# All pages of cached values issued from GpSimd's queue, two per unit behind the visit that frees the ring

## The reference

```python
def fox_sample(q, k_new, v_new, logf_new, cache_k, cache_v, cache_logf, page_table):
    DB, DS = q.shape[:2]
    P = page_table.shape[1] * PAGE_SIZE
    k_past = cache_k[page_table].reshape(DB, P, N_HEADS, HEAD_DIM)
    v_past = cache_v[page_table].reshape(DB, P, N_HEADS, HEAD_DIM)
    ...
    s = jnp.einsum('bqhd,bkhd->bhqk', q, k_all, preferred_element_type=jnp.float32) * HEAD_DIM ** -0.5
    s = s + (Fh[..., P:, None] - Fh[..., None, :])
    ...
    p = jax.nn.softmax(s, axis=-1)
    out = jnp.einsum('bhqk,bkhd->bqhd', p.astype(v_all.dtype), v_all)
    return out.reshape(DB, DS, ATTN_WIDTH)
```

## Time and profile before

| what | value |
|---|---|
| three runs | 1341.45 us median (1341.02 to 1342.53) |
| the profiled execution | 1339.1 us, its span 1337.3 us |
| TensorE busy | 1295.2 us, 97% of the span |
| VectorE, ScalarE, GpSimd busy | 689.0, 401.7, 607.0 us |
| granted TensorE clock | 0.993 over the span |
| cached values, issues from SyncE | 256 of 256 KB, 3.3 us median from issue to landing |

### The profile page before, as it was taken

How to read it: one execution, slowest core, us unless ns; L and a number is a source line. 1 busy time by engine, 2 the same in 40 slices (tenths; PEclk the granted TensorE clock), 3 DMA queues, 4 the chain that set the end, 5 groups by cost and what they waited for, 6 DMA issues and landing times. The chain is left out here.

```text
span 1337.3 us, 21207 instructions
## 1 busy us (share of the span) xinstructions
PE 1295.2 (97%) x7573; PEld 1035.9 (77%) x7573; DVE 689.0 (52%) x1049; ACT 401.7 (30%) x589; POOL 607.0 (45%) x286
## 2 busy tenths in 40 slices
PE   8999999999899999999999999999999999999996
PEld 6889898988799976777777777677777776666675
DVE  4765555534577654636446384645545234321438
ACT  3546666664521341121212112121211202112016
POOL 1027877753400438565666655676672112121114
PEclk9999999999999999999999999999999999999999
DMA  7344545330254157777687867778685544567633
GB/s 243 104 145 150 170 158 158 127 99 1 89 188 152 36 161 252 256 258 238 232 262 244 279 225 246 237 239 281 198 288 168 200 137 175 191 267 282 236 128 127
DMA packets 111538, 255.02 MB, mean 191 GB/s; under 512 B 12624, under 2 KB 22737, under 8 KB 106048
## 3 DMA queue, kind: packets, MB, share of 16 engines
q1 hardware_dynamic: 102152, 246.99, 54.9%
q10 hardware_dynamic: 8320, 4.19, 1.1%
q0 software_dynamic: 960, 2.47, 0.6%
HBM read 243.72 MB, written 10.12 MB: 190 GB/s over the span
## 5 line engine op out<-in xcount | busy, mean ns | idle before, releaser
L886 POOL TENSOR_TENSOR WL<-WR,WH 128x1024 fp32r<-128x1024 f32 x55 | 133.0, 2419 | 336.3 <-ACT WH L1122 336.3
L794 POOL TENSOR_TENSOR AR<-AR,QB 128x1024 f32<-128x1024 f32 x96 | 235.1, 2465 | 107.5 <-DMA AR<-cache_k 93.4
L1548 PE MATMUL PSM<-XH,WH 128*128 128x512 f32 x672 | 213.4, 399 | 0.0
L1548 PE MATMUL PSM<-XL,WH 128*128 128x512 f32 x672 | 208.0, 391 | 0.0
L1548 PE MATMUL PSM<-XH,WL 128*128 128x512 f32 x672 | 207.0, 389 | 0.0
L2139 DVE TENSOR_TENSOR ACC<-ACC,PSM 128x512 f32<-128x512 f32 x160 | 108.6, 684 | 133.5 <-PE PSM L1558 133.1
L1122 ACT CAST WH<-WR 128x1024 fp32r<-128x1024 f32 x55 | 57.6, 1049 | 354.2 <-PE PSM L1548 186.0
L1548 PEld LDWEIGHTS PSM<-XH,WH 128*128 128x128 f32 x672 | 121.9, 188 | 50.4 <-issue 27.6
L1558 PE MATMUL PSM<-R 128*128 128x512 f32 x528 | 148.4, 390 | 0.1
L1548 PEld LDWEIGHTS PSM<-XH,WL 128*128 128x128 f32 x672 | 126.2, 188 | 27.3
L1548 PEld LDWEIGHTS PSM<-XL,WH 128*128 128x128 f32 x672 | 126.1, 188 | 27.3
(11 more groups left out here) (281 smaller groups left out, 2187.7 us busy)
## 6 DMA issues: line engine op xcount, KB each, us to landing
AR<-cache_v SPq DMA_DIRECT2D x256, 256.0 KB, 3.3
AR<-cache_k SPq DMA_DIRECT2D x192, 256.0 KB, 3.5
AR<-ws SPq DMA_DIRECT2D x37, 1024.0 KB, 6.4
WR<-ffn SPq DMA_DIRECT2D x66, 512.0 KB, 4.9
WR<-w_in SPq DMA_DIRECT2D x20, 512.0 KB, 4.7
ACC<-cache_k SPq DMA_DIRECT2D x32, 256.0 KB, 2.8
WR<-cache_k SPq DMA_DIRECT2D x32, 256.0 KB, 3.1
WR<-w_o SPq DMA_DIRECT2D x5, 1024.0 KB, 5.1
```

The source lines that it names most:

```text
L794: pool.tensor_tensor(keys, keys, QB[:].rearrange("p (o n) -> p o n", o=1).to_broadcast([P, KP, AW]), ALU.mult).then_inc(k_mul, 1)
L886: pool.tensor_tensor(lo, WR[:, raw_weight(e), :], hi.bitcast(F32), ALU.subtract).then_inc(ffn_lo, 1)
L1548: ins = pe.matmul(out[:, hc], (hi, lo)[a][:, k * P:(k + 1) * P], x[b][:, k, hc], start=(k == 0 and n == 0), stop=(k == KC - 1 and n == 2))
```

## The change

SyncE's program loses all issues of values. GpSimd's program gets them: `value_pages(n, first)` reads two page numbers of chunk n, waits for `v_used` to reach n - 1 (from the third chunk on), and issues the two DMAs. `VPAGE` places four such calls behind each visit, one in each of the next four units: two for the first of the two chunks, two for the second. In a unit they stand behind the rests and ahead of the multiply. The first two chunks (four calls) go out behind the rests of the first two weight tiles. 128 calls stand in GpSimd's program in all.

```diff
-VLOAD = tuple(o + n for o in VALUES for n in (1, 2))
+VPAGE = {b * WIN + o + 1 + n: (b * NCH + 2 * i + 2 + n // 2, 2 * (n % 2)) for b in range(NB) for i, o in enumerate(VALUES)
+         for n in range(CH) if b * NCH + 2 * i + 2 < NB * NCH}
...
             sp.wait_ge(o_free, HRT * OC)
-            pages(0, VR, 0, t["cache_v"], v_ld)
-            pages(1, VR, 1, t["cache_v"], v_ld)
             sp.wait_ge(wo_lo, OC + 1)
...
-                if u == (NB - 1) * WIN + VLOAD[-1]:
+                if u == (NB - 1) * WIN + VALUES[-1] + 2:
                     stream_tile(2)
...
-                for c in range(2, NCH + 2):
-                    n = b * NCH + c
-                    if o == VLOAD[c - 2] and n < NB * NCH:
-                        pages(n, VR, n % 2, t["cache_v"], v_ld, v_used, n - 1)
...
+            def value_pages(n, first):
+
+                numbers = [pool.value_load(page[0:1, bass.ds(n * CH + j, 1)], min_val=0, max_val=POOL_PAGES - 1)
+                           for j in (first, first + 1)]
+                if n >= 2:
+                    pool.wait_ge(v_used, n - 1)
+                for j, p in enumerate(numbers, first):
+                    pool.dma_start(VR[n % 2][:, j * AW:(j + 1) * AW],
+                                   t["cache_v"][bass.ds(p, 1), :, :].rearrange("a p n -> (a p) n")).then_inc(v_ld[n % 2], 16)
+
+            pool.wait_ge(o_free, HRT * OC)
+            for n in range(2):
+                for first in (0, 2):
+                    value_pages(n, first)
             for u in range(UNITS):
                 for e in range(2, len(WORDER)):
                     if WORDER[e][2] + 1 == u:
                         rest(e)
+                if u in VPAGE:
+                    value_pages(*VPAGE[u])
                 if u in KMUL:
                     multiply(EARLY + KMUL.index(u))
```

## The result

The changed kernel takes 1363.32 us (median of 4 runs, 1359.79 to 1366.24) against 1341.24 us for the kernel before, measured beside it: a ratio of 1.0167 (95% interval 1.0136 to 1.0198), **22 us slower**. The forecast was 1340.2 us, in a range from 1338.4 to 1362. The profiled execution took 1364.32 us around a span of 1362.6 us, 25.3 us more than before.

The account below looks back on a forecast made before the run. TensorE was taken to bound the kernel: 2.9 us of its stalls for cached values go, 1.4 + 0.2 come, net 1.3 us gained, so 1340.2 us on the median's scale. Whole range 1338.4 to 1362, the forecast's own 1338.5 to 1342.5.

Parts of the forecast that it names:

- The bound and what there is to gain: TensorE, 485 to 1100 us: only its delays cost time; two waits for late pages of values, 2.9 us at most.
- Price of an issue: GpSimd's queue: 0.62 us a page, between 0.542 and 1.03; at about 0.7 the new stalls reach 2.9 us.
- GpSimd's load: GpSimd, per period of 50 units: 32 pages add 19.8 us to 49.6, making 69.4 of 78 us, 89%.
- It fits: GpSimd's queue: the added load fits with little slack; elsewhere calls and landing take 16.3 us, inside 17.1 between visits.
- First chain: Visit at 522.1 us: last call ends at 520.3 to 521.3, landing 3.3 to 4.0 later; TensorE waits 1.4 us.
- Second chain: Visit at 742.9 us: last call ends at 740.3, pages land at 743.6 to 744.3; wait 0 to 0.4, taken 0.2.
- First eight pages: Start of GpSimd's page issues, 461.0 us: first multiplies delayed by 5 us, first reader at 485.8, so no cost.
- VectorE's waits: VectorE waiting for GpSimd's multiplies, 85.8 us already: one or two us more at some of them cost nothing.
- The third: GpSimd's queue between visits: issue at 0.8 us, ten visits late by 1.2 us each, 9 us lost, 1350.5; chance 0.20.
- The second rival: DMA engines, busy for 0.72 of the stretch: traffic keeps late pages late, no change, 1341.45 us; chance 0.10.
- The fourth: GpSimd becomes the bound: register loads in series, 1.03 us a page, 82.6 us in 78; 30 us lost, 1372; chance 0.18.
- The 0.05 for an unseen loss: Unspecified place, such as a late multiply holding up VectorE's sums: some 3 to 10 us lost; chance 0.05.

Follow-up runs that it names:

- act_first_sync: Against the change: the calls for pages of values stand in ScalarE's program instead of GpSimd's, the first eight pages go out from SyncE; 1337.53 us (0.9978).
- sync_values_first: Against the kernel before: in SyncE's program the pages of values stand ahead of the unit's weight tile and pages of keys; 1338.69 us (0.9971).
- half_split: Against the change: GpSimd issues only the second chunk behind each visit, SyncE the first in the unit behind the visit; 1348.62 us (1.0064).
- pool_constant_pages: Against the change: GpSimd's page numbers of values are constants (4n + j) instead of register loads from the page table; 1357.12 us (1.0108).
- dg_psum: Against the change: dg stays on VectorE but reads the 8x8 identity from PSUM instead of SBUF; 1358.91 us (1.0119).

## Why the prediction was wrong, step by step

- **The bound and what there is to gain: right.** Only TensorE's delays cost time, and about 2.9 us were to be gained: act_first_sync and sync_values_first got 3.6 and 2.8 us.
- **Price of an issue: too low by 0.09 us.** 0.62 us were taken. Measured are 0.536 and, spread over 256 pages, 45.1 us of register gaps, 0.18 us: 0.71, just the break-even named (0.7). By the prediction's own sum the price alone would have made neither a gain nor a loss. But the gaps are not spread: they are 1.16 us a call where calls follow each other, which is behind a wait for a visit, when the queue is already late.
- **GpSimd's load: right.** 69.4 us of work in a period of 78, 89%, were forecast. In the period from 897 to 975 us, which has no halt, GpSimd is busy for 66.2 us (the fifth engine in the row) and stands for 4.2 before calls, 70.4 in all. The 548.5 of 615 us above are also 89%, but by chance: they hold 37.4 us of waiting, which no forecast of work counts.

```profile
897.00:975.00 78.00, 78.00 (x380) 58.00 (x378) 46.86 (x50) 13.13 (x14) 66.19 (x53) 1.00 0.76 248
```

- **"It fits": wrong, the first step that failed.** What was left was taken for slack to catch up with. It is spent in waits for casts (62.4 us) at fixed places. Lateness was followed in two chains, and "Elsewhere four calls with three multiplies or subtractions among them ... are 16.3 us, inside the 17.1 us" was said of the rest. Six visits of 31 were late. By the trace's records the last issue ended 1.3, 2.5 and 1.4 us before the start of those at 522.60, 613.05 and 783.99 us, too late even for a landing of 4.0; at the other three it ended 3.2 to 4.7 us before and the landing alone made the wait.
- **First chain: issue right, landing wrong.** The last call was forecast to end at 520.3 to 521.3 and ended at 521.28, at the late end. Its pages were to land 3.3 to 4.0 us later and took 5.6 and 6.7 from the ends of their issues; so the wait was 4.39 us, not 1.4. This is the term that was wrong most. The two bounds are medians, which the views count from the start of an issue, and the prediction added them to its end. From the end the change's pages take 3.8 us at the median, inside the bounds (SyncE's took 3.0); but the last page took 4.3 to 7.1 us at the six late visits. With 4.0 there the same issues would have made some 4 us of waits instead of 11.8 (an estimate from the records). From 514.8 to 520.8 us SyncE, now free of values, issued six pages of keys and a weight tile beside GpSimd's pages, and the DMA share is 0.97 and then 1.02 in the windows above. Counted over the trace's records, a page lands (median, from the end of its issue) after 2.4 us with no other transfer in flight, 3.9 with three, 4.3 with five and 6.3 with eight; before there were never more than five, now up to ten. act_first_sync has the same dependence (2.4, 3.5, 4.6, 6.0). No run held the number in flight down with GpSimd as the issuer, so this is a dependence in two traces and not a test. The Trainium skill ("DMA: Bandwidth & Descriptors", "Issuing engines are not separate DMA queues") says that all issuers share the 16 DMA engines, and these runs agree; the prediction's reading of it, that the landing stays at today's, was wrong, for a second issuer puts more in flight.
- **Second chain: wrong by 1.6 us.** Waits of 0 to 0.4 us were forecast at the second visit of that sample; its second half, at 767.81 us, waited for 1.77, again for pages that took up to 6.0 us from the end of the issue.
- **First eight pages: right for the change** (its first visit is at 486.09 us, 485.85 in the kernel before), though half_split and pool_constant_pages, with other timing, reach that visit 3.6 and 9.9 us late.
- **VectorE's waits, "I cost at nothing too": wrong, the second step that failed.** The prediction looked at multiplies that VectorE waits for; these waits grew only from 85.8 to 93.1 us. What came was VectorE's own instructions on SBUF lasting until GpSimd's run ends: 6.9 us of TensorE's waiting for `dg`, and VectorE's 47.3 us (counted as what its instructions from 485 to 1100 us take beyond the shortest of their form: 49 us before, 98 after). The Trainium skill ("SBUF — State Buffer", "Who interferes with whom") gives the lock between the two engines, which the prediction cited in the other direction: VectorE holding up GpSimd's issues. By the trace that costs nothing (536 ns at the median, 597 at most). By the same section an instruction of VectorE with at most one input in SBUF, outside its two-port modes, is free of the lock; dg_psum agrees (0.214 us at most).
- **The clock: missing from the sum.** 8.4 us follow the halts and come on top of the 15.8 us of new waits, about half as much again. Not every halt costs it: from 765 to 805 us TensorE waits for 1.77 and 1.89 us at two visits, and the granted clock is 1.00.
- **The rivals.** The third named a dearer issue (0.8 us), which is not there, but its ending, some ten late visits, is the nearest: six, 11.8 us. That its 12 us of waits come so close is luck, as its cause is not there and its time, 1350.5 us, is 13 too low. The second rival's traffic is in the landing. The fourth named register work in series as what would make GpSimd the bound. GpSimd keeps the period from 897 on, yet register work is part of the loss: 4 to 6 us by two runs for the loads, 20.8 us with all that the constants changed. The 0.05 for an unseen loss "that holds VectorE's sums up" was the right engine with the wrong mechanism, and too small a chance.

## What to carry to other kernels

A helper engine whose work fills nine tenths of its time has no slack if the rest is waits at fixed places: count what each late instruction makes late on other engines, not only the load, and add the clock that a halt of TensorE can take afterwards. Where a page leaves just ahead of its use, reckon with a late landing and not with the median. Register work for dynamic addresses is free only behind a running instruction, so calls in a row pay for it; give them to a queue that computes little. Before moving work to another engine, try the order within the queue where it is: one move in SyncE's program got what the change was to get.

## What was not expected of the hardware

- A VectorE instruction with its operands in SBUF can be kept waiting through several of GpSimd's instructions that follow each other without a gap: 8.61 us instead of 1.27 beside three multiplies, 9.58 instead of 1.20 beside two rests, a multiply and the issues behind them, up to 10.38 for an 8 x 8 product of 0.22 us. With its tensor operand in PSUM the same product took 0.214 us at most. It isn't so at every boundary: in the change's trace VectorE got in between two rests at 752.9 us, and the second took 3.38 us instead of 2.39. What decides is not shown.

```profile
750.53 2.39 POOL L881 TENSOR_TENSOR WL<-WR,WH 128x1024 fp32r<-128x1024 f32 x1 [1.86 <-ACT WH L1133]
752.87 3.38 POOL L881 TENSOR_TENSOR R<-WR,R 128x1024 fp32r<-128x1024 f32 x1
...
752.37 1.63 DVE L2141 TENSOR_TENSOR R<-AR,R 128x1024 fp32r<-128x1024 f32 x1 [1.74 <-ACT R L1175]
```

- 256 issues of 8 KB each on GpSimd take 0.522 us apiece, those of 256 KB 0.536: the price hardly depends on the bytes. Both have 128 rows; whether it goes with the rows no run here shows.
